# Latent attention's scores as rounded passes on row halves, in pairs of units

## The reference, cut to what matters

```python
q = (rmsnorm_2(cq, g_cq) @ w_uq).reshape(b, s, MLA_HEADS, MLA_NOPE + MLA_ROPE)   # 8 heads, 64 + 32
kv = (rmsnorm_2(ckv, g_ckv) @ w_ukv).reshape(b, s, MLA_HEADS, MLA_NOPE + MLA_V)
qa = jnp.concatenate([qa_n, rope_2d(qa_r, row_pos, col_pos)], axis=-1)
ka = jnp.concatenate([ka_n, jnp.broadcast_to(ka_r, ka_n.shape[:-1] + (MLA_ROPE,))], axis=-1)
# keys: 512 tokens and 256 of the context; the rotary key is one for all heads
sc = jnp.einsum('bqhd,bkhd->bhqk', qblk, k, preferred_element_type=jnp.float32) * scale   # 96 ** -0.5
p = jax.nn.softmax(sc, axis=-1).astype(v.dtype)
o = jnp.einsum('bhqk,bkhd->bqhd', p, v)
```

## Time and profile before

| | us |
|---|---|
| three runs | 1866.73, 1869.57, 1870.66 (median 1869.57) |
| the profiled execution | 1870.87, its span 1869.1 |
| TensorE busy | 1706.1 (91%) |
| VectorE, ScalarE, GpSimd busy | 609.1, 470.8, 268.7 |
| set-up of the latent attention | 1404.5 to 1434.3 |
| its loop, first scores to last scores | 1434.3 to 1522.9 |

### The profile page before, as it was taken

The page is one execution under the profiler, slowest core; times in us unless marked ns, Lnnn a source line. Parts: engine busy times, 40 slices in busy tenths (PEclk is TensorE's granted clock), DMA queues, the critical chain, the costliest instruction groups (busy, mean ns, idle before and its releaser), DMA issues.

```text
span 1869.1 us, 21461 instructions
## 1 busy us (share of the span) xinstructions
PE 1706.1 (91%) x8783; PEld 1013.3 (54%) x8783; DVE 609.1 (33%) x1080; ACT 470.8 (25%) x902; POOL 268.7 (14%) x115
## 2 busy tenths in 40 slices
PE   7999999889989898888988889899899999999998
PEld 5797577653342432424324233243495668878876
DVE  4796783550020200202002020020366540260055
ACT  5236725320000100001000010000344442353232
POOL 3342621000000000000000000000230014106470
PEclk9999999999999999999999999999999999999999
DMA  8333043349999999999999999999810005203121
GB/s 329 132 125 92 35 158 158 136 180 398 428 428 430 427 430 428 427 430 427 427 431 427 429 429 427 430 428 428 316 45 1 1 9 116 91 9 119 72 83 45
DMA packets 64541, 484.22 MB, mean 259 GB/s; under 512 B 10236, under 2 KB 16853, under 8 KB 38751
## 3 DMA queue, kind: packets, MB, share of 16 engines
q1 hardware_dynamic: 64479, 483.36, 63.9%
HBM read 480.94 MB, written 2.41 MB: 259 GB/s over the span
## 4 chain that ended last, share of the span: by engine, by line
PE 72%; DMA 16%; DVE 6%; ACT 3%; issue 3%; POOL 0%; DVEq 0%; ACTq 0%; SPq 0%
PE psum L528 26%; PE psum L1799 17%; DMA ring<-in_expert_w_down 13%; PE psum L1819 7%; PE psum L1782 4%; PE psum L644 3%; PE psum L679 3%; PE psum L1828 3%; DMA ring<-in_expert_w_gu 3%; PE psum L657 2%; PE psum L2450 2%; PE psum L1485 1%; DVE small L745 1%; PE psum L669 1%; DVE work_area L1872 1%
## 5 line engine op out<-in xcount | busy, mean ns | idle before, releaser
L1799 PE MATMUL psum<-ring,work_area 128*64 128x512 f32 x2048 | 448.3, 594 | 34.2 <-DMA ring<-in_expert_w_gu 26.4
L1799 PEld LDWEIGHTS psum<-ring,work_area 128*64 128x64 f32 x2048 | 148.3, 137 | 327.6 <-issue 276.9
L1819 PE MATMUL psum<-ring,work_area 128*64 128x512 f32 x1024 | 232.9, 609 | 16.9 <-DMA ring<-in_expert_w_down 14.9
L1889 DVE TENSOR_TENSOR work_area<-psum,work_area 128x512 f32<-128x512 f32 x32 | 20.6, 686 | 593.5 <-ACT work_area L1852 593.5
L1819 PEld LDWEIGHTS psum<-ring,work_area 128*64 128x64 f32 x1024 | 75.2, 140 | 163.6 <-issue 143.9
L2036 POOL TENSOR_TENSOR hn<-x_res,ring 128x1024 f32<-128x1024 f32 x3 | 9.0, 3009 | 1022.2 <-DVE x_res L1896 1022.2
L1852 ACT ACTIVATE work_area<-psum 128x512 f32<-128x512 f32 x32 | 17.4, 594 | 484.0 <-PE psum L1799 484.0
L1948 POOL TENSOR_TENSOR block_lo<-ring,part_hi 128x1024 fp32r<-128x1024 f32 x36 | 89.5, 2499 | 291.6 <-ACT part_hi L1941 291.5
L528 PE MATMUL psum<-h_hi,part_hi 128*128 128x512 f32 x256 | 99.8, 390 | 1.0 <-DVE hn L796 1.0
L528 PE MATMUL psum<-h_hi,block_lo 128*128 128x512 f32 x256 | 99.6, 389 | 0.0
L528 PE MATMUL psum<-h_lo,part_hi 128*128 128x512 f32 x256 | 99.6, 389 | 0.0
(11 more groups left out here) (436 smaller groups left out, 2724.7 us busy)
## 6 DMA issues: line engine op xcount, KB each, us to landing
ring<-in_expert_w_gu SPq DMA_DIRECT2D x128, 2048.0 KB, 27.2
ring<-in_expert_w_down SPq DMA_DIRECT2D x64, 2048.0 KB, 21.3
ring<-in_w_in SPq DMA_DIRECT2D x12, 2048.0 KB, 8.1
extra<-in_w_mod SPq DMA_DIRECT2D x4, 1536.0 KB, 9.2
ring<-in_w_out SPq DMA_DIRECT2D x3, 2048.0 KB, 13.9
ring<-in_ca_wkv SPq DMA_DIRECT2D x1, 4096.0 KB, 16.1
ring<-in_w_in SPq DMA_DIRECT2D x3, 1024.0 KB, 20.3
hn<-in_w_mod SPq DMA_DIRECT2D x2, 1536.0 KB, 8.5
```

The lines of the kernel that those rows point to most:

```text
L1799: ins = pe.matmul(psum[h * 64:(h + 1) * 64, c, :], xsT[:, k, e * CAP:(e + 1) * CAP], w[:, (2 * c + h) * BANK:(2 * c + h + 1) * BANK], star ...
L1819: ins = pe.matmul(psum[n * 64:(n + 1) * 64, 6, :], hidT[b][:, j, h, :], w[:, j, n * BANK:(n + 1) * BANK], start=(q == 0 and j == 0), stop= ...
```

## The change

The scores of the latent attention are built from rounded parts. The 64 own features of two heads lie one above the other on row halves; high and rest are kept for keys (`kn_hi`, `kn_lo`) and queries (`qn_hi`, `qn_lo`). The 32 rotary features are copied threefold, 96 rows: for the keys rounded, rest, rounded; for the queries rounded, rounded, rest. One product over the 96 rows is the sum of three passes. A unit's scores are now four products per segment, and `step=2` issues them for the two heads in turn. The scale 96^-0.5 is multiplied into the q gain earlier (`router_gain_dve`). The set-up computes the rotary q in token rows (256 columns for a tile) and the other q directly turned, onto column halves; ScalarE makes all rounded parts, VectorE subtracts all rests and releases the banks, and ScalarE now copies the values. The diff, cut to its core:

```diff
@@ attention @@
+            score_passes = passes or (lambda h, qt: [(at, [(q_at(h, qt), keys)]) for at, keys in k_at(h, qt)])
@@ scores_pe @@
-                for s in range(len(pieces[0])):
-                    for u in range(first, first + step):
-                        c, qt, j = units[u]
-                        if s == 0 and u >= n_scores:
-                            pe.wait_ge(exped, before + u - n_scores + 1)
-                        at, keys = pieces[u - first][s]
-                        ins = pe.matmul(at(score_at(u)), q_at(heads[c][j], qt), keys, start=True, stop=True)
+                for s, (_, sides) in enumerate(pieces[0]):
+                    for m in range(len(sides)):
+                        for u in range(first, first + step):
+                            if s == 0 and m == 0 and u >= n_scores:
+                                pe.wait_ge(exped, before + u - n_scores + 1)
+                            at, sides = pieces[u - first][s]
+                            queries, keys = sides[m]
+                            ins = pe.matmul(at(score_at(u)), queries, keys, start=(m == 0), stop=(m == len(sides) - 1))
...
@@ mla_in_dve @@
+            dve.tensor_copy(kr_copies, ckv[:, :, KV_LORA:].unsqueeze(2).to_broadcast([P, KT2, 3, ROPE])).then_inc(sem("kr"), 1)
@@ mla_up_pe @@
-            for i, g in enumerate(g_q):
-                t, n = i // 2, i % 2
+            for i, g in enumerate(g_qr):
                 B.acquire(pe, g)
-                B.filled(product(g, B.at(g)[:, 0:384], [(cqT[:, c, t * P:(t + 1) * P], uq[:, c, n * 384:(n + 1) * 384])
-                                                       for c in range(2)]), g)
+                for t in (2 * i, 2 * i + 1):
+                    ins = product(g, B.at(g)[:, t % 2 * 256:t % 2 * 256 + 256].rearrange("p (h c) -> p h c", h=MLA_H),
+                                  [(cqT[:, c, t * P:(t + 1) * P], uq[:, c, :].rearrange("p (h c) -> p h c", h=MLA_H)[:, :, NOPE:])
+                                   for c in range(2)])
+                B.filled(ins, g)
...
+            for i, g in enumerate(g_qn):
+                B.acquire(pe, g)
+                for c in range(2):
+                    for j in range(2):
+                        h = 2 * i + j
+                        ins = pe.matmul(B.at(g)[j * NOPE:(j + 1) * NOPE, :], uq[:, c, h * QK_MLA:h * QK_MLA + NOPE], cqT[:, c, :],
+                                        start=(c == 0), stop=(c == 1), skip_group_check=True)
+                B.filled(ins, g)
             pe.wait_ge(sem("q_rot"), T)
...
@@ mla_up_act: rounded keys, then values, then q @@
+            for i, g in enumerate(g_kn):
+                B.full(act, g)
+                v = kn_of(kn_hi, i)
+                act.activation(v, B.at(g)[:, 0:v.shape[1]], ACT.Identity).then_inc(h2_rounded, 1)
+            for t, g in enumerate(g_va):
+                B.full(act, g)
+                B.release(copy(act, va[:, t, :], B.at(g)), g)
+            for i, g in enumerate(g_qn):
+                B.full(act, g)
+                act.activation(qn_hi[:, i, :], B.at(g), ACT.Identity).then_inc(h2_rounded, 1)
...
@@ mla_up_dve: four rotated tiles stand ahead of the keys' rests @@
+                link(rotate_halves(v, c, s))
+                dve.tensor_copy(q_copies[:, t], q_rope[:, t].unsqueeze(2).to_broadcast([P, MLA_H, 3, ROPE])).then_inc(sem("q_rot"), 1)
+            for i, g in enumerate(g_kn):
+                dve.wait_ge(h2_rounded, KN + i + 1)
+                v, high = kn_of(kn_lo, i), kn_of(kn_hi, i)
+                B.release(dve.tensor_tensor(v, B.at(g)[:, 0:v.shape[1]], high.bitcast(F32), ALU.subtract), g)
...
@@ the passes @@
+        def mla_passes(h, qt):
+            i, rows, q = h // 2, slice(h % 2 * NOPE, h % 2 * NOPE + NOPE), slice(qt * P, (qt + 1) * P)
+            qh, ql, qr = qn_hi[rows, i, q], qn_lo[rows, i, q], qr_parts[0:3 * ROPE, h, q]
+            def segment(lo, hi):
+                kh, kl = kn_hi[rows, i, lo:hi], kn_lo[rows, i, lo:hi]
+                return (lambda score: score[:, lo:hi]), [(qh, kh), (qh, kl), (ql, kh), (qr, kr_parts[0:3 * ROPE, lo:hi])]
+            return [segment(lo, hi) for lo, hi in KEY_SEGS]
...
-            besides={(act, 24): lambda: round_part(PART["kb"])})
+            step=2, besides={(act, 24): lambda: round_part(PART["kb"])}, passes=mla_passes)
```

More of the change, by code:

```diff
@@ L634, in scores_pe @@
             def scores_pe(first):
-                pieces = [k_at(heads[units[u][0]][units[u][2]], units[u][1]) for u in range(first, first + step)]
-                for s in range(len(pieces[0])):
-                    for u in range(first, first + step):
-                        c, qt, j = units[u]
-                        if s == 0 and u >= n_scores:
-                            pe.wait_ge(exped, before + u - n_scores + 1)
-                        at, keys = pieces[u - first][s]
-                        ins = pe.matmul(at(score_at(u)), q_at(heads[c][j], qt), keys, start=True, stop=True)
-                        if s == len(pieces[0]) - 1:
-                            ins.then_inc(scored, 1)
+                pieces = [score_passes(heads[units[u][0]][units[u][2]], units[u][1]) for u in range(first, first + step)]
+                for s, (_, sides) in enumerate(pieces[0]):
[6 more added lines that the diff above has]
+                            ins = pe.matmul(at(score_at(u)), queries, keys, start=(m == 0), stop=(m == len(sides) - 1))
+                            if s == len(pieces[0]) - 1 and m == len(sides) - 1:
+                                ins.then_inc(scored, 1)
             def turn_pe(u):
@@ L2154, in build @@
         g_cqT = B.take(2)
-        g_q = B.take(2 * T)
+        g_qr = B.take(2)
         g_kn = B.take(MLA_H)
         g_va = B.take(KT2)
-        g_qT2 = B.take(MLA_H)
+        g_qn = B.take(MLA_H // 2)
+        g_qrT = B.take(MLA_H)
         KEY_SEGS = ((0, S), (S, NTOK))
@@ L2209, in mla_up_act @@
                 B.release(copy(act, cqT[:, c, :], B.at(g), g_cq_col[:, c:c + 1]), g)
-            for i, g in enumerate(g_q):
-                t, n = i // 2, i % 2
+            for i, g in enumerate(g_qr):
                 B.full(act, g)
-                B.release(copy(act, q_tok[:, t, 4 * n:4 * n + 4, :], B.at(g)[:, 0:384].rearrange("p (h c) -> p h c", h=4),
-                               QK_MLA ** -0.5), g)
-            key_drain(act, 0)
-            for h, g in enumerate(g_qT2):
-                if h % 2 == 0:
-                    B.full(act, g)
-                    B.release(copy(act, qT_mla[:, h, :], B.at(g)[0:QK_MLA, :]), g)
@@ L2221, in key_drain @@
-        def key_drain(eng, seg):
-            lo, hi = KEY_SEGS[seg]
-            for i, g in enumerate(g_kn[seg::2]):
-                B.full(eng, g)
-                for j in range(2):
-                    ins = copy(eng, kT_mla[0:NOPE, 2 * i + j, lo:hi], B.at(g)[j * NOPE:(j + 1) * NOPE, 0:hi - lo])
-                B.release(ins, g)
-        def mla_up_dve():
-            for g, (lo, hi) in zip(g_krT, KEY_SEGS):
-                B.full(dve, g)
-                B.release(dve.tensor_copy(kT_mla[NOPE:QK_MLA, :, lo:hi],
-                                          B.at(g)[0:ROPE, 0:hi - lo].unsqueeze(1).to_broadcast([ROPE, MLA_H, hi - lo])), g)
+                B.release(copy(act, q_rope[:, 2 * i:2 * i + 2].rearrange("p t h c -> p (t h c)"), B.at(g)), g)
@@ new lines, in mla_up_act @@
+            for h, g in enumerate(g_qrT):
+                B.full(act, g)
+                act.activation(qr_parts[0:3 * ROPE, h, :], B.at(g)[0:3 * ROPE, :], ACT.Identity).then_inc(h2_rounded, 1)
+        def mla_up_dve():
+            lo_rows = slice(ROPE, 2 * ROPE)
+            for i, (g, (lo, hi)) in enumerate(zip(g_krT, KEY_SEGS)):
+                dve.wait_ge(h2_rounded, KR + i + 1)
+                v = kr_parts[lo_rows, lo:hi]
+                B.release(dve.tensor_tensor(v, B.at(g)[lo_rows, 0:hi - lo], v.bitcast(F32), ALU.subtract), g)
```

73 lines of the change are left out of this document (44 added, 29 removed).

## The result

| | before | after |
|---|---|---|
| median | 1869.26 us (1866.73 to 1870.66) | 1924.51 us (1918.10 to 1927.32, four runs) |
| ratio, 95% interval | | 1.0292 [1.0262, 1.0323] |
| the profiled execution, its span | 1870.87, 1869.1 | 1918.10, 1916.4 |
| TensorE's granted clock, mean of that span | 0.984 | 0.974 |
| set-up: first transposes to first scores | 29.8 | 38.4 |

The account below looks back on a forecast made before the run. It took TensorE to bound the set-up and a latency chain with two units in flight the loop. Loop +33.5 and set-up +9 made +42.5 us on 1870.87: 1913.4, at the median 1912 us; range 1892 to 1938.

Parts of the forecast that it names:

- the pair's ring of waits: Latent attention loop: next scores wait for both exponentials and a ScalarE copy behind them; lost overlap outweighs what tiling saves.
- the forecast case: Whole kernel: the forecast of 1912 us holds, bracket 1900 to 1922 us, chance 0.47.
- rival 1: Loop: TensorE's clock falls to half after each round's hole; +18 us, 1930 us; bracket 1922 to 1945, chance 0.20.
- part 2: Loop under step=2: a pair's round 6.47 us against 4.30, +2.17 in each of 14; loop +33.5 us.
- S: Loop: time of a pair's scores on TensorE, 2.49 to 2.85 us, taken as 2.65; outer ends 1.73 and 3.54.
- part 1: Loop scores: halves overlap, four layout changes cost 0.19 us each; a pair's scores take 2.65 us.
- The first two pairs: Loop start, no stalled transposes: S + 3.06 us each, together 11.4 against 8.29, so +3.1 us.
- part 3: Set-up: VectorE's draining stalls TensorE 5.4 us between keys and values; +9 us, from +4 to +11.
- No overlap: Loop scores: rounded passes on row halves don't overlap, S = 3.54; +57 us, 1926 us; chance 0.11.
- free switches: Loop and set-up: layout changes cost nothing, set-up +4; +23 us, 1892 us; bracket 1888 to 1900, chance 0.16.
- faster: Loop: TensorE's work is the bound, a pair 3.05 us against 4.30; about -9 us, 1861 us; chance 0.04.
- Later stages: Stages behind the loop: they shift with the loop's end and give no time back.

Follow-up runs that it names:

- takers_only: Kernel after, with VectorE instead of ScalarE taking the first and third of a unit's turned pieces; 1899.33 us, ratio 1.0153.
- f32_pairs: Kernel before, its f32 scores run in pairs of units (step=2), nothing rounded; 1902.21 us, ratio 1.0177.
- two_switches: Kernel after, 96-row pass first at 512 columns and last at 256, so two layout changes a pair instead of four; 1922.11 us, ratio 1.0281.
- rounded_single: Kernel after without step=2: rounded passes for one unit at a time; 1920.70 us, ratio 1.0267.
- full_rows_single: Kernel after without step=2, its half-row passes widened to all 128 rows (scores not the reference's); 1881.38 us, ratio 1.0067.
- halves_apart: Kernel after, with one head's three half-row passes, then the other's, then both 96-row passes; 1933.46 us, one run.
- best_form: Kernel after with two layout changes a pair, key rests taken earlier in the set-up, and VectorE as first taker of turned pieces; 1884.00 us, ratio 1.0076.
- f32_pairs_vector_first: Kernel before with its f32 passes, run in pairs (step=2) and with VectorE as first taker of turned pieces; 1879.86 us, ratio 1.0052.

## Why the prediction came out as it did

The mechanism named as decisive, the pair's ring of waits, is shown, and the time lies in the range. The bracket of the forecast case was 1900 to 1922, and 1924.5 lies just above it, in that of rival 1, the clock. That the forecast came as near as 12.5 us is in part luck: it put set-up and loop at 42.5 us where the rows show 36.4 (8.6 and 27.8), and left out some 16 us of the clock in the loop. By its steps:

- **The round (part 2)** was forecast as S + 3.82. Measured: 6.33 with S = 2.45, S + 3.88. That the last piece waits for both exponentials through ScalarE's copy is shown by takers_only, which takes 0.88 us out by moving this copy alone, and that it is the pairs' doing by f32_pairs. Rounds with an output product came as forecast: 9.49 for 9.6. But the last pair, counted as a fourteenth round with +2.17, costs only 0.9 us more than the two last units before.
- **S (part 1)** was 2.45 instead of 2.65, 14 x 0.20 = 2.8 us over all. The overlap of the halves is there. The layout change costs 0.2 (two_switches; 0.19 was taken). The Trainium skill ("TensorEngine Tiling (Array Packing)", Key Properties) says that changing the tiling mode drains TensorE; the trace agrees as far as the 0.2 us go. The weight loads of two half passes are hidden even in 0.12 us: in the kernel after passes of 256 columns start 0.12 apart (1462.94 and 1463.06). It was the lower end, 2.49, that was right.
- **The first two pairs (part 2)** were put at S + 3.06 each, with both maxima ahead of the next pair. The trace shows that the next pair's first product waits for the first exponential alone: it starts at 1445.01, 1.86 us after the scores before it, and only the second head's waits for the second. At full clock the two pairs would take some 9.9 us (estimated above), not 11.4.
- **The set-up (part 3)**: 8.6 us for 9. The stall was 4.2 for 5.4, because the threefold copies took 0.56 us and not 0.7, and the front waited 1.54 us. What the stall was shorter the clock made up: at 0.50 behind it the values took 7.11 us for 5.4, which wasn't foreseen. The first scores came at 1438.7 and not at 1443.5, of which 4.3 us are the earlier stages of this execution.
- **The clock** was the mis-sized term: nothing in the forecast, 15.6 us in the profiled execution. Rival 1 had it, at 18 us, with a chance of 0.20. Its way of counting, two thirds of the rounds with their scores at half clock, isn't what happened: that was so in 4 of 14 rounds, and the first two pairs, the output products and the transposes paid the rest. So its 18 us lie near by chance. Its counter-evidence was one hole at 407 after which the clock stayed up; the nearer row was the fall at 1437 after the hole in front of the loop itself. The 36.4 us make 1906, and with the clock of the profiled execution 1922; the 3 us up to the median are not placed.
- **No overlap, free switches, faster** are out: S is neither 3.54 nor 1.73, and the chain does not consist of TensorE. The last came true in an unforeseen place: in rounded_single TensorE is the bound, and it is slower than the kernel before all the same (1920.70 us).
- **Later stages** gave back 0.5 us, as forecast nothing.

What stays open: why the clock returns so much later on half rows than on full ones, whether the layout changes have a part in it, and how the clock's 15.6 us divide between holes and half rows.

## What to carry to other kernels

Before putting two units of a softmax loop side by side, write down for each buffer that comes round again which engine's copy frees it and what stands ahead of that copy in the engine's list: here one copy behind two exponentials cost 0.9 us a round, and giving it to the other engine was worth 7 us even in the kernel before. Here a new form of the scores could gain nothing, since the chain of the pairs was made of waits: with the f32 passes the round was 6.14 us, with the rounded ones 6.33. And price each new hole of TensorE twice, once for itself and once for the clock of the passes behind it.

## What the runs showed of the hardware

- TensorE's clock stood at 0.50 for 51 us while TensorE was busy 10.00 of 10 us, on passes of 64 and 96 rows with full-row transposes between them (rounded_single). With the 64-row passes on 128 rows, and so without layout changes, it was back after 6 us (full_rows_single).
- Passes of two row halves overlap even when the second half's stand three places later in the list (halves_apart: both start at 1495.82, the first head's second pass at 1496.16).
- A change between the half-row and the full layout costs 0.2 us at full clock (two_switches: 0.41 for two).
- With holes of 2.2 us in each round the clock fell back to 0.50 five times behind its first stretch (after), with holes of 1.92 us eight times (f32_pairs, full-height passes), with holes of 1.28 us not at all behind the first 23 us (takers_only) or once, near the end (best_form, between 1535 and 1545), with holes of 0.96 us never (f32_pairs_vector_first).
- A copy 128x768 within the local memory took VectorE 0.56 us, a rest 32x512 from PSUM 0.68, as long as a full 128x512 (0.69; both means of the kernel after).
